# Hybrid decoder trunk: the rotary swap of the attention layer by DMA instead of TensorE, v taken out of PSUM by ScalarE, and the index search spread differently over the units

## What is computed

```python
def apply_partial_rope(x, cos, sin):
    half = ROPE_DIM // 2
    x1, x2, rest = x[..., :half], x[..., half:ROPE_DIM], x[..., ROPE_DIM:]
    return jnp.concatenate([x1 * c - x2 * s, x2 * c + x1 * s, rest], axis=-1)

def dsa_attention(q, k, v, q_idx, k_idx, w_idx, top_k):   # one block of 128 queries
    score = jax.nn.relu(jnp.einsum('bthd,bsd->bths', qib, k_idx))
    score = jnp.einsum('bths,bth->bts', score, wb)
    _, sel = lax.top_k(jnp.where(admissible[None], score, -jnp.inf), top_k)
    ... softmax over the selected keys, times v

def conv_sparse_attn_mixer(h, cos, sin, w_in, conv_w, w_out, top_k):
    sc_b, sc_c, sc_x, q, k, v, q_idx, k_idx, w_idx = split_cols(h @ w_in, ...)
    y_conv = sc_b * causal_depthwise_conv(sc_c * sc_x, conv_w)
    q, k, q_idx, k_idx = apply_partial_rope of each
    y_attn = dsa_attention(q, k, v, q_idx, k_idx, w_idx * const, top_k)
    return jnp.concatenate([y_conv, y_attn], axis=-1) @ w_out
```

## Time and profile before

| | |
|---|---|
| median of 3 runs | 2097.87 us (2097.70 to 2098.47) |
| the profiled execution | 2097.97 us |
| its span, first to last instruction | 2096.2 us |
| PE busy | 2066.4 us, 99% of the span |
| DVE busy | 1046.1 us, 50% |
| ACT, POOL busy | 770.6 and 298.0 us |
| mean granted PE clock | 0.999 of full speed |
| intervals 1 to 28 of the mixer | 373.37 to 602.57 us of the span |

### The profile page before, as it was taken

One profiled execution on the slowest core, in us unless ns is written; L12 is line 12 of the kernel. 1 busy time (PEld: TensorE's weight loads), 2 busy tenths in 40 slices (PEclk: granted clock), 3 DMA queues, 4 the chain that ended last, 5 costly groups with the idle time before them and its releaser, 6 DMA issues.

```text
span 2096.2 us, 25750 instructions
## 1 busy us (share of the span) xinstructions
PE 2066.4 (99%) x9608; PEld 1705.8 (81%) x9608; DVE 1046.1 (50%) x1551; ACT 770.6 (37%) x1086; POOL 298.0 (14%) x384
## 2 busy tenths in 40 slices
PE   9999999999999999999999999999999999999998
PEld 7888888777778888888888888878888888888887
DVE  5444444489744444433344442366767554444423
ACT  5333222333754333322333332254555553333222
POOL 0000000443221000000000000036565110000000
PEclk9999999999999999999999999999999999999999
DMA  5333322462123333322332332222122223233321
GB/s 188 94 100 93 119 97 74 126 166 85 57 72 99 92 99 100 109 97 86 91 98 92 100 113 97 82 88 92 48 92 60 79 91 99 92 100 96 115 97 54
DMA packets 62972, 200.39 MB, mean 96 GB/s; under 512 B 12560, under 2 KB 14640, under 8 KB 62896
## 3 DMA queue, kind: packets, MB, share of 16 engines
q1 hardware_dynamic: 60256, 198.72, 30.4%
q10 hardware_dynamic: 2640, 0.65, 0.1%
HBM read 188.58 MB, written 2.38 MB: 91 GB/s over the span
## 4 chain that ended last, share of the span: by engine, by line
PE 84%; DVE 9%; ACT 3%; issue 2%; POOL 1%; DMA 1%; SPq 0%; ACTq 0%; DVEq 0%; POOLq 0%
PE prod L497 25%; PE prod L499 25%; PE prod L498 25%; PE misc L766 2%; DVE top L1369 1%; DVE qc L1629 1%; DVE raw L1370 1%; ACT w_hi L929 1%; PE misc L713 1%; DVE w_lo L1231 1%; PE prod L561 0%; PE prod L562 0%; PE prod L565 0%; DVE kc L1629 0%; DVE raw L1362 0%
## 5 line engine op out<-in xcount | busy, mean ns | idle before, releaser
L1231 DVE TENSOR_TENSOR w_lo<-raw,w_hi 128x1024 fp32r<-128x1024 f32 (+1 forms) x290 | 383.7, 1323 | 741.2 <-ACT w_hi L929 740.2
L497 PE MATMUL prod<-h_hi,w_hi 128*128 128x512 f32 x1848 | 738.8, 400 | 0.7 <-DVE w_lo L1231 0.3
L499 PE MATMUL prod<-h_hi,w_lo 128*128 128x512 f32 x1848 | 721.3, 390 | 0.0
L498 PE MATMUL prod<-h_lo,w_hi 128*128 128x512 f32 x1848 | 720.2, 390 | 0.0
L929 ACT ACTIVATE w_hi<-raw 128x1024 fp32r<-128x1024 f32 (+1 forms) x316 | 354.8, 1123 | 561.2 <-PE prod L499 546.5
L499 PEld LDWEIGHTS prod<-h_hi,w_lo 128*128 128x128 f32 x1848 | 347.1, 188 | 74.0
L497 PEld LDWEIGHTS prod<-h_hi,w_hi 128*128 128x128 f32 x1848 | 347.5, 188 | 72.9 <-issue 4.5
L498 PEld LDWEIGHTS prod<-h_lo,w_hi 128*128 128x128 f32 x1848 | 347.7, 188 | 69.5 <-issue 2.9
L497 PE MATMUL prod<-a_hi,w_hi 128*128 128x512 f32 x682 | 265.3, 389 | 0.0
L498 PE MATMUL prod<-a_lo,w_hi 128*128 128x512 f32 x682 | 265.3, 389 | 0.0
L499 PE MATMUL prod<-a_hi,w_lo 128*128 128x512 f32 x682 | 265.3, 389 | 0.0
(11 more groups left out here) (303 smaller groups left out, 1880.4 us busy)
## 6 DMA issues: line engine op xcount, KB each, us to landing
raw<-in_w SPq DMA_DIRECT2D x252, 512.0 KB, 3.5
raw<-in_wd SPq DMA_DIRECT2D x64, 704.0 KB, 4.1
blk<-blocks SPq DMA_DIRECT2D x16, 256.0 KB
x<-in_x SPq DMA_DIRECT2D x8, 256.0 KB, 4.8
k_dup<-act_f SPq DMA_DIRECT2D x8, 256.0 KB, 4.1
k_dup<-silu_g SPq DMA_DIRECT2D x8, 256.0 KB, 4.1
silu_g<-g_rows SPq DMA_DIRECT2D x7, 256.0 KB, 4.8
out<-y_out SPq DMA_DIRECT2D x12, 128.0 KB, 1.9
```

The source lines that it names most:

```text
L497: pe.matmul(bank, wh, hi, start=first and k == 0, stop=False)
L498: pe.matmul(bank, wh, lo, start=False, stop=False)
L499: ins = pe.matmul(bank, wl, hi, start=False, stop=last and k == tiles_n - 1)
L1231: dve.tensor_tensor(w_lo[:, n % 2, 0:w], raw[:, n % 4, 0:w], w_hi[:, n % 2, 0:w].bitcast(F32), ALU.subtract).then_inc(lo_ready, 1)
```

## The change

- **Rotary swap by DMA.** The columns of iq, ik, k and q are reordered on the way in, so that the two channels that rotate together stand on neighbouring partitions (8n and 8n + 1); `rope_frequencies` carries the sign. DVE makes the sine product first and signals it (`sine_ready`); in slot 1 ACT issues two DMAs that copy 16 partitions of 512 numbers each (`swap_act`, 32 KB each) from `turned_in` to `swapped`, crosswise; the other rows of `swapped` were set to zero once by POOL. DVE waits for both (`swap_in`) in slot 6 and adds. The twelve matmuls of `rot` are gone; `hf` has one buffer for the product and one for the swap.
- **v on ACT.** ACT takes the bank out (slot 0, ahead of the weight split) and writes `vtok` in four activations with a factor per token (slot 5). That factor comes from PE in interval 2: four matmuls with one moving column turn `rstd` to tokens.
- **Convolution.** POOL squares `rstd` once, DVE multiplies c by the square, and the second multiplication (L1452) is gone. The two shifted steps of x stand in slots 6 and 7, not 4 and 6.
- **Search.** The index pieces stand in intervals 5 to 10 (slots 2 and 5) in another order, each added on DVE in slots 6 and 7 of the same interval. Each waits only for the copy of its own unit. The 48 rounds are placed by a table (`TOP_PLACES`) over intervals 8 to 24: five in each of 14 to 17, one or two in most of the others.

```diff
+IDX_ORDER = [(1, 0), (1, 1), (2, 0), (1, 2), (2, 1), (1, 3), (2, 2), (2, 3), (3, 0), (3, 1), (3, 2), (3, 3)]
+IDX_FROM, IDX_PLACES, ADD_PLACES = 5, (2, 5), (6, 7)
+TOP_PLACES = {8: (2, 4), 9: (2, 4), 10: (2, 4), 11: (1, 2, 4), 12: (1, 2, 4), 13: (2, 4, 7), 14: (1, 2, 4, 5, 7),
+              15: (1, 2, 4, 5, 7), 16: (1, 2, 4, 5, 7), 17: (1, 2, 4, 5, 7), 18: (2, 5, 7), 19: (2, 7), 20: (2, 7),
+              21: (2, 7), 22: (2, 7), 23: (5,), 24: (5,)}
...
-    idx = [("idx", b, j) for b in range(1, TT) for j in range(PAIRS)]
-    top = [("top", b, r) for b in range(1, TT) for r in range(ROUNDS)]
-    out = {}
-    for u in range(len(EV_UNITS)):
-        for k in (3, 6):
-            if u >= 7 and idx:
-                out[u * KT + k] = [idx.pop(0)]
-        for k in (2, 4, 5, 7) if 14 <= u < 18 else (2, 5, 7):
-            if u >= 9 and top:
-                out[u * KT + k] = [top.pop(0)]
...
+    index, add, top = {}, {}, {}
+    for i, pair in enumerate(IDX_ORDER):
+        u = IDX_FROM + i // 2
+        index[u * KT + IDX_PLACES[i % 2]] = pair
+        add[u * KT + ADD_PLACES[i % 2]] = pair
+    rounds = [(b, r) for b in range(1, TT) for r in range(ROUNDS)]
+    for u, places in TOP_PLACES.items():
+        for k in places:
+            top[u * KT + k] = rounds.pop(0)
...
-        roped_in = hf
+        turned_in, swapped = hf[:, 0, :], hf[:, 1, :]
...
             def idx_pe(b, j):
-                p = (b - 1) * PAIRS + j
+                p = IDX_ORDER.index((b, j))
                 if p == 0:
                     pe.wait_ge(rlo_ready, 1)
-                    pe.wait_ge(stacked[0], 2 * STACKED)
-                    pe.wait_ge(stacked[1], 2 * STACKED)
                 else:
                     pe.wait_ge(relu_done, p)
+                pe.wait_ge(stacked[(j + 1) % 2], STACKED * (j // 2 + 1))
                 w = (b + 1) * P
...
+                    for t in range(TT):
+                        at = TT * HEADS + t
+                        ins = pe.matmul(misc[:, 2, at:at + 1], rstd[:, t * P:(t + 1) * P], const["ident"][:, 0:1],
+                                        start=True, stop=True)
                     ins.then_inc(rot_done, 1)
-                elif kind in ROPED:
-                    pe.wait_ge(evac, EV_S + u + 1)
-                    pe.wait_ge(roped, u)
-                    pe.matmul(misc[:, 0, :], const["rot"], roped_in[:, u % 2, :], start=True, stop=True)\
-                        .then_inc(rot_done, 1)
...
+            def swap_act(v):
+
+                act.wait_ge(sine_ready, v)
+                act.wait_ge(roped, v)
+                if v == 1:
+                    act.wait_ge(swap_zero, 1)
+                for x1, x2 in ((0, 1), (1, 0)):
+                    act.dma_start(swapped[x1:P:8], turned_in[x2:P:8]).then_inc(swap_in, 16)
+
+            def v_act(v, k):
+
+                m = EV_UNITS[v][1]
+                if k == 0:
+                    act.wait_ge(unit_done, EV_N + v + 1)
+                    act.wait_ge(evac, EV_S + v)
+                    if m < 2:
+                        act.wait_ge(roped, V_FIRST)
+                    else:
+                        act.wait_ge(rot_done, m)
+                    act.activation(hf[:, v % 2, :], prod[:, 2 * ((EV_S + v) % 2), :], ACT.Copy).then_inc(evac, 1)
+                elif k == 5:
+                    act.wait_ge(rot_done, m + 2)
+                    for t in range(TT):
+                        ins = act.activation(vtok[:, t, m, :], misc[:, 0, t * P:(t + 1) * P], ACT.Copy,
+                                             scale=rstd_tok[:, t:t + 1])
+                    ins.then_inc(roped, 1)
...
+                    if kind == "v":
+                        v_act(u - 1, k)
                     if k == 0 and u > 1:
                         split(EV_N + u + 1)
+                    if k == 1 and kind in ROPED:
+                        swap_act(u - 1)
...
+                    dve.wait_ge(swap_in, 32 * u)
                     dve.wait_ge(evac, EV_S + u + 1)
-                    dve.tensor_tensor(dst, dst, misc[:, 0, :], ALU.add).then_inc(roped, 1)
-                elif kind == "v":
-                    dve.wait_ge(rot_done, u + 1)
-                    dve.tensor_copy(vtok[:, :, m, :], tiles(misc[:, 0, :])).then_inc(roped, 1)
+                    dve.tensor_tensor(dst, dst, swapped, ALU.add).then_inc(roped, 1)
...
+                if k == 0 and kind != "v":
                     dve.wait_ge(unit_done, EV_N + u + 1)
                     if u == 0:
                         dve.wait_ge(rstd_ready, 2)
-                    if kind in ("ik", "iq", "k", "q", "v"):
-                        if u < 2:
-                            dve.wait_ge(trig_ready, 2)
+                        dve.wait_ge(trig_ready, 2)
+                        dve.tensor_tensor(turned_in, bank, rstd[:], ALU.mult).then_inc(evac, 1)
+                    elif kind in ROPED:
+                        if u == 1:
+                            dve.wait_ge(rot_done, 1)
+                        elif u == 2:
+                            dve.wait_ge(rlo_ready, 1)
                         else:
-                            dve.wait_ge(rot_done, u - 1)
-                            dve.wait_ge(roped, u - 1)
-                        if kind in ROPED:
-                            if u == 2:
-                                dve.wait_ge(rlo_ready, 1)
-                            elif u >= 3:
-                                dve.wait_ge(stacked[u % 2], STACKED * ((u - 1) // 2))
-                            dve.tensor_tensor(split_hl[u % 2][:, 1, :], bank, cosT[:], ALU.mult)
-                            dve.tensor_tensor(roped_in[:, u % 2, :], bank, sinT[:], ALU.mult).then_inc(evac, 1)
-                        else:
-                            dve.tensor_tensor(roped_in[:, u % 2, :], bank, rstd[:], ALU.mult).then_inc(evac, 1)
+                            dve.wait_ge(stacked[u % 2], STACKED * ((u - 1) // 2))
+                        dve.tensor_tensor(turned_in, bank, sinT[:], ALU.mult).then_inc(sine_ready, 1)
+                        dve.tensor_tensor(split_hl[u % 2][:, 1, :], bank, cosT[:], ALU.mult).then_inc(evac, 1)
                     elif kind == "c":
-                        dve.tensor_tensor(cbuf[:], bank, rstd[:], ALU.mult).then_inc(evac, 1)
+                        if m == 0:
+                            dve.wait_ge(r2_ready, 1)
+                            dve.wait_ge(evac, EV_S + u)
+                        dve.tensor_tensor(cbuf[:], bank, rstd_2[:], ALU.mult).then_inc(evac, 1)
+                        dve.wait_ge(evac, EV_S + u + 1)
...
-                elif kind == "c" and k == 2:
-                    dve.wait_ge(evac, EV_S + u + 1)
-                    link(dve.tensor_tensor(cbuf[:], cbuf[:], rstd[:], ALU.mult))
...
-                elif kind == "x" and k in (4, 6):
-                    j = k // 2 - 1
+                elif kind == "x" and k in (6, 7):
+                    j = k - 5
...
-                elif k == (7 if u <= 1 else 5):
+                elif k == (7 if u <= 1 else 6) and (kind == "ik" or kind in ROPED):
...
+                    if v == V_FIRST - 1:
+                        pool.tensor_tensor(rstd_2[:], rstd[:], rstd[:], ALU.mult).then_inc(r2_ready, 1)
...
+    for n in range(HD // 8):
+        rot[8 * n + 1, 8 * n] = rot[8 * n, 8 * n + 1] = -1.0
...
+    sign = np.where(row % 8 == 0, 1.0, np.where(row % 8 == 1, -1.0, 0.0))
+    return (sign * f[row // 8]).astype(np.float32)[:, None]
+
+
+def head_order():
+
+    half, order = HD // 8, np.zeros(HD, np.int64)
+    order[0::8], order[1::8] = np.arange(half), np.arange(half, 2 * half)
+    order.reshape(-1, 8)[:, 2:] = np.arange(2 * half, HD).reshape(-1, 6)
+    return order
...```

What stands where on DVE in interval 10 (it finishes unit 9, the first q), from the sine or cosine product on. Before:

```order
L1437 TENSOR_TENSOR act_f<-prod,cosT 128x512
L1438 TENSOR_TENSOR hf<-prod,sinT 128x512
L1362 SCALAR_TENSOR_TENSOR raw<-probsT,w_idx,raw 128x384 x2
L1369 MAX top_67<-raw 128x8
L1370 MATCH_REPLACE raw<-top_67,raw 128x256
L1391 TENSOR_TENSOR act_f<-act_f,misc 128x512
L1369 MAX top_67<-raw 128x8
L1370 MATCH_REPLACE raw<-top_67,raw 128x256
L1362 SCALAR_TENSOR_TENSOR raw<-sq,w_idx,raw 128x384 x2
```

129 lines of the change are left out of this document (63 added, 66 removed).

## The result

The changed kernel takes **2108.85 us** (median of 5 runs, 2108.60 to 2110.24) against 2097.87 before. The ratio is 1.0052, with a 95% interval of 1.0038 to 1.0067. It is 11 us slower, where 14 us faster had been forecast.

What follows compares the result with a forecast made beforehand. PE was taken as the bound (busy 99% of the span, 84% of the chain). Terms -10.3 - 3.5 - 2.1 + 0.8 + 1.9 + 1.4 + 1.6 - 4.0 = -14.2 gave 2083.7 us for the median, range 2077 to 2094.

Steps and rivals of the forecast that it cites:

- Rotations, -10.3: PE in the mixer: twelve rotations of 0.86 us each taken off PE, -10.3 us.
- Waits at rotations (-3.5) and v (-2.1): PE's waits for the sine product at the last five rotations and for DVE's evacuation at v transposes both go.
- Start, intervals 2 to 5.: Small records delay DVE's side work and `w_lo` of units 3 to 5 comes later: +1.9 us (0.9 to 4).
- Intervals 5 to 10: PE waits once late swaps in four of six intervals use up the cushion: +1.4 us (0 to 6).
- third rival: Six search intervals: score additions wait for both POOL steps, ring grows 3.3 us each, +19.8, 2103.5 us; chance 6%.
- the ring: DVE from sine to sine, intervals 5 to 10: 2.2 + L plus score additions, 6.3 to 7.7 us against PE's 6.4 to 7.3.
- L: Time from the second swap DMA's start to landing: 2.1 us, 3.0 in k intervals, ends 1.9 and 3.7.
- The cushion.: Intervals 5 to 10: lateness up to about 2 us is free, since PE's second index piece in slot 5 needs the first relu.
- Intervals 11 to 16, +1.6: ACT's ring leaves 0.2 us and POOL squares `rstd` ahead of a `w_lo`; lateness carried in: +1.6 us (0 to 4).
- Search and attention, -4.0: DVE loses 12 steps and is off the chain until 548 after one early wait; PE's waits go: -4.0 us (0 to -7).
- The rule weighed.: Engines alternate between SP's and ACT's rings packet by packet, so L stays near 2.1 everywhere, sum some 2 us lower.
- Signs to look for.: No L669, interval 3 near 6, pair additions of 2 us and more for third rival, landing median above 2.6: forecast too low.

Runs made afterwards that it cites:

- old_places: Changed kernel, swap kept, with index pieces, score additions and search rounds back in the places of the kernel before: 2106.2 us.
- pool_late: Changed kernel, but POOL starts its low half in intervals 5 to 10 only behind the score additions: 2091.6 us.
- rounds_first: Changed kernel with both pairs of score additions ahead of the rotary addition and search rounds of intervals 9 and 10 at places 1 and 2: 2089.6 us.
- adds_ahead: Changed kernel with score additions moved on DVE: first pair ahead of the rotary addition, second behind the next interval's cosine product: 2094.1 us.
- copies_late: Changed kernel, but SP issues a unit's stacked copies and the weight loads behind them only when the next unit's swap has landed: 2103.7 us.
- turn_on_pe: Changed kernel with the swap alone undone, so the matrix product on PE turns the channels again: 2097.3 us.
- half_copies: pool_late with each k unit's stacked copies carrying the high half alone (4 x 128 KB, not 4 x 256 KB); output not the wanted one: 2084.0 us.
- turn_on_pe_old_places: Changed kernel with the swap undone (matrix product on PE) and the search in the places of the kernel before: 2097.2 us.

## Why the prediction was wrong, step by step

- **Rotations, -10.3: right in size, not in effect.** An undisturbed roped interval without index pieces is 5.44 us where it was 6.35 (interval 5 of old_places, 11 of pool_late): 0.91 each, 0.86 predicted. Eight more small records: interval 2 took 9.18 us instead of 8.32, +0.86 (+0.8 predicted). Waits at rotations (-3.5) and v (-2.1): in pool_late PE waits 0.2 us in all from interval 11 to 16, so both can go; v intervals 14 to 17 took 24.6 us where 24.0 were forecast, in rounds_first 23.7.
- **Start, intervals 2 to 5.** Predicted: four rotations less (-3.4), +0.8, +1.9, so -0.7. Measured -0.4, with two index pieces of 0.5 us moved into interval 5, so -1.4 without them. Near enough.
- **"Intervals 5 to 10", +1.4 (0 to 6): the step that failed.** Intervals 6 to 10 got 20.4 us longer although five rotations had left them. Three things were wrong in it. (1) *The additions* were taken at 2.0 to 3.4 us for two pairs; they took 4.9 to 6.0. The price of POOL's hold stood in the third rival almost right (3.3 a turn of the ring, 2.9 measured), but its chance of 6% rested on the sentence that the last additions find `w_lo` running only with lateness above 1 us. In the first search interval that is so at once: unit 5 ends at 407.27, which releases the split of unit 7, and POOL's low half starts at 407.81, so its `w_lo` (409.06) follows without a gap and the additions, from 406.99 to 411.93, meet both. And it feeds itself, since held additions make the next sine late. (2) *L* was taken at 3.0 in the k intervals; the second swap DMA landed in 4.3 to 5.3, above the upper end of 3.7. Over all 24 swap DMAs the median is 2.8, above the 2.6 that the prediction had named as its limit. (3) *The clock* was in no term: 6.3 us of slow product steps. Even the third rival's 2103.5 is 5 us short, since it priced the hold without a later landing and without the clock.
- **The cushion.** "Lateness up to about 2 us is free" was used for L alone. The rivals were priced one by one, while the late landing (1.3 to 2.3 us above the value taken) and the hold (2.9) stand in the same ring and add up. adds_ahead takes the additions out of the ring and pool_late the hold, and they get 19 and 15 of the 20 us in intervals 6 to 10 back; copies_late, with landings of 1.8 to 2.6 and the hold left, gets 8. In the first two most landings shortened of themselves, since a sine that is less late issues its swap ahead of the copies. What the runs show is that both members are needed: with the hold removed (pool_late) 15 of the 20 us go, and with the landing removed (turn_on_pe) 15 to 16. The share of each can't be told apart.
- **The copies' loop** was in no step. The prediction had the k unit's 1 MB of copies as traffic beside the swap, not as something that a sine waits for; half_copies prices the two together at 7.6 us.
- **Intervals 11 to 16, +1.6.** They took 45.0 us before, and three rotations, four index pieces and the waits at rotations and v left them. They came to 40.1 in the changed kernel and 35.1 in pool_late; PE waited 4.3 us in them in the first (1.1, 2.6 and 0.7, in 12, 13 and 15), where +1.6 was forecast, and 0.2 in the second. The rings forecast for 3, 4, 11 and 12 did fit: intervals 3 and 11 are 6.3, interval 4 5.9.
- **Search and attention, -4.0 (0 to -7).** Intervals 17 to 28 gave 2.7. With the old places they gave 1.1 (turn_on_pe_old_places), so 1.6 to 2.3 is the new places' share.
- **The rule weighed.** The swap's landing was 1.8 to 1.9 us with nothing of SP's in flight and 4.3 to 5.3 beside k copies, so the copies do hold it up, and "L stays near 2.1 everywhere" does not hold. The same section of the Trainium skill ("DMA: Bandwidth & Descriptors", queues, rings and completion order) also says that a DMA's semaphore increment lands only after every earlier write of that DMA engine, across its queues; that is hardly needed for the landings of 4 to 5 us. In the changed kernel's trace the last packet of the second swap DMA ends 0.4 to 0.7 us before the landing in intervals 7 to 10 (439.9 and 440.3 in interval 8) and 0.3 before it in intervals 2, 3 and 5. So all but 0.1 to 0.4 of the delay lies in packets that start late.
- **Signs to look for.** Right were: no L669, interval 3 near 6, score additions over 2 us as the mark of the third rival, the landing's median as the mark of the sum.

## What to carry to other kernels

Price the waits of one ring together: a step that costs nothing by itself (a longer landing within the cushion) and another that costs nothing by itself (an addition that POOL may hold) can close a loop in which each makes the other happen. When an operation leaves the bottleneck engine for a DMA, look at what else is in flight at that moment and who reuses the buffers it reads; here a wait on POOL or another place for the additions was worth 15 to 19 us, and the swap itself nothing beside the full copies. Before a matrix product is taken off PE, first see that PE would not just wait there: with the rotation on PE and a clean order, the kernel has no wait left in this stretch and is as fast.

## What the runs showed of the hardware

- **Which DVE steps POOL holds.** Beside POOL's steps, additions that read two tensors from SBUF wait for POOL's end (4.20 us for a pair, 1.27 alone). So does the rotary addition, now that its second operand is in SBUF: 1.68 us in the changed kernel beside `w_lo`, where the same addition with that operand in PSUM took 0.69 beside `w_lo` in the kernel before. (In the earlier trace rows it starts just behind the POOL step, so that row does not show it.) The search steps are not held. In order: the rotary addition and the POOL step beside it in the changed kernel, then the two in the kernel before.

```profile
405.38 1.68 DVE L1425 TENSOR_TENSOR silu_g<-silu_g,hf 128x512 f32<-128x512 f32 x1 [1.82 <-DMA hf<-hf]
...
404.12 2.39 POOL L1728 TENSOR_TENSOR w_lo<-raw,w_hi 128x1024 fp32r<-128x1024 f32 x1
```

```profile
391.97 2.39 POOL L1696 TENSOR_TENSOR w_lo<-raw,w_hi 128x1024 fp32r<-128x1024 f32 x1
392.90 0.69 DVE L1391 TENSOR_TENSOR silu_g<-silu_g,misc 128x512 f32<-128x512 f32 x1 [1.74 <-PE misc L669]
```

Two search steps in adds_ahead, with the POOL step that they stand beside; 0.42 and 0.41 us are their times without one too.

```profile
462.84 0.42 DVE L1402 MAX8 top<-raw 128x8 f32<-128x256 f32 x1
...
463.38 0.41 DVE L1403 MATCH_REPLACE8 raw<-top,raw 128x256 f32<-128x256 f32 x1
...
462.47 1.29 POOL L1737 TENSOR_TENSOR silu_g<-silu_g 128x512 fp32r<-128x512 f32 x1 [5.30 <-ACT silu_g L1115]
```

- **A small DMA beside large ones.** 32 KB on ACT's queue landed in 1.7 to 1.9 us alone. The second of two landed in about 2.8 beside 128 KB copies, and in 4.3 to 5.3 beside 256 KB copies and a 512 KB load.
- **The clock after a wait.** In the changed kernel the five waits of 2.0 to 4.0 us in intervals 6 to 10 were each followed by 3 to 9 product steps at 1.2 GHz, and one of 2.6 us in interval 13 by none; one of 2.0 us in interval 13 of rounds_first was followed by nine, and those of 2.0 and 2.1 us in interval 8 of pool_late and rounds_first by none. Which waits bring the clock down can't be read from their length alone.
